# A two-layer decoder step: other places for the attention's products, the convolution's mean, the queries' normalisation and one parked slab

## What is computed

```python
x = x + 0.5 * swiglu_ffn(rmsnorm(x, ffn1_norm), w_gate, w_up, w_down)
cols = rmsnorm(x, mix_norm) @ w_in                       # 512 conv, 1152 attention, 640 rwkv
y_a = conv_module(glu(cols_a), conv_w, ...)              # 31 taps, layer norm over 256 channels, silu
y_b = combine_dilations(dilated attention over 3 groups) # samples: over cached windows wink, winv too
y_c, S = rwkv_time_mix(cols_c, prev, S0, ...)            # delta-rule recurrence, done in chunks
x = x + concat([y_a, y_b, y_c]) @ w_out
q = rmsnorm(x, xattn_norm) @ w_q
mk, mv = split(rmsnorm(mem, mem_norm) @ w_kv)            # samples use caches mem_k, mem_v instead
x = x + softmax(q mk^T / 16) mv @ w_o
x = x + 0.5 * swiglu_ffn(rmsnorm(x, ffn2_norm), ...)
```

## Time and profile before

| | |
|---|---|
| median of three runs | 1671.87 us |
| profiled execution | 1671.88 us |
| its span | 1670.1 us |
| PE busy | 1593.0 us (95%) |
| VectorE busy | 1074.7 us (64%) |
| ScalarE busy | 753.5 us (45%) |
| POOL busy | 207.1 us (12%) |
| transfers | 303.71 MB, 182 GB/s in the mean |

### The profile page before, as it was taken

One profiled execution on the slowest core, in us unless ns is written; L12 is line 12 of the kernel. 1 busy time (PEld: TensorE's weight loads), 2 busy tenths in 40 slices (PEclk: granted clock), 3 DMA queues, 4 the chain that ended last, 5 costly groups with the idle time before them and its releaser, 6 DMA issues.

```text
span 1670.1 us, 32138 instructions
## 1 busy us (share of the span) xinstructions
PE 1593.0 (95%) x13716; PEld 1507.9 (90%) x13716; DVE 1074.7 (64%) x1659; ACT 753.5 (45%) x1293; POOL 207.1 (12%) x190
## 2 busy tenths in 40 slices
PE   8999999999899989999999999998998998999997
PEld 8999999886689779999999999998767896999997
DVE  6776467878563367775477754779875642777744
ACT  5444348324444344443354433573355443544433
POOL 1000000980010010000010000029501000100000
PEclk9999999998999999999999999999979999999999
DMA  6666744303537665445445667442234477544541
GB/s 241 268 248 249 290 161 135 113 20 90 215 117 291 257 252 177 156 172 168 161 159 209 237 254 275 135 149 72 61 120 177 152 287 301 198 173 154 175 164 41
DMA packets 39965, 303.71 MB, mean 182 GB/s; under 512 B 4816, under 2 KB 4976, under 8 KB 7408
## 3 DMA queue, kind: packets, MB, share of 16 engines
q1 hardware_dynamic: 37488, 288.92, 47.8%
q0 software_dynamic: 2048, 11.17, 2.4%
q10 hardware_dynamic: 288, 1.57, 0.3%
HBM read 291.88 MB, written 36.83 MB: 197 GB/s over the span
## 4 chain that ended last, share of the span: by engine, by line
PE 79%; DVE 11%; ACT 5%; DMA 2%; issue 2%; SPq 0%; DVEq 0%; ACTq 0%
PE bank L676 22%; PE bank L678 22%; PE bank L677 21%; PE bank L860 3%; DVE w_lo L1911 3%; ACT w_hi L1385 1%; DMA slots<-stream 1%; ACT arena L1385 1%; PE bank L1285 1%; PE bank L1270 1%; DVE h_mem L1927 1%; PE bank L1339 1%; PE bank L1158 1%; PE bank L824 1%; PE bank L1322 1%
## 5 line engine op out<-in xcount | busy, mean ns | idle before, releaser
L1911 DVE TENSOR_TENSOR w_lo<-slots,w_hi 128x1024 fp32r<-128x1024 f32 x386 | 484.5, 1258 | 339.5 <-ACT w_hi L1385 338.5
L676 PE MATMUL bank<-h_hi,w_hi 128*128 128x288 f32 x1936 | 578.1, 299 | 18.3 <-DVE w_lo L1911 10.5
L677 PE MATMUL bank<-h_lo,w_hi 128*128 128x288 f32 x1936 | 571.9, 295 | 0.0
L678 PE MATMUL bank<-h_hi,w_lo 128*128 128x288 f32 x1936 | 570.0, 294 | 0.0
L1385 ACT CAST w_hi<-slots 128x1024 fp32r<-128x1024 f32 x390 | 406.4, 1046 | 290.0 <-PE bank L678 261.4
L676 PEld LDWEIGHTS bank<-h_hi,w_hi 128*128 128x128 f32 x1936 | 363.6, 188 | 25.9 <-DVE w_lo L1911 10.2
L678 PEld LDWEIGHTS bank<-h_hi,w_lo 128*128 128x128 f32 x1936 | 365.3, 189 | 0.0
L677 PEld LDWEIGHTS bank<-h_lo,w_hi 128*128 128x128 f32 x1936 | 364.3, 188 | 0.3
L678 PE MATMUL bank<-hid_hi,w_lo 128*128 128x288 f32 x704 | 207.7, 295 | 0.0
L677 PE MATMUL bank<-hid_lo,w_hi 128*128 128x288 f32 x704 | 207.3, 294 | 0.0
L676 PE MATMUL bank<-hid_hi,w_hi 128*128 128x288 f32 x704 | 207.1, 294 | 0.0
(11 more groups left out here) (334 smaller groups left out, 2115.6 us busy)
## 6 DMA issues: line engine op xcount, KB each, us to landing
slots<-stream SPq DMA_DIRECT2D x237, 1024.0 KB, 5.0
out_win3k<-win3k SPq DMA_DIRECT2D x2, 4080.0 KB
out_win3v<-win3v SPq DMA_DIRECT2D x2, 4080.0 KB
h_mem<-stream SPq DMA_DIRECT2D x4, 1024.0 KB, 10.6
out_win2k<-win2k SPq DMA_DIRECT2D x2, 2032.0 KB
out_win2v<-win2v SPq DMA_DIRECT2D x2, 2032.0 KB
con<-consts SPq DMA_DIRECT2D x1, 2340.0 KB, 10.8
arena<-mem_in POOLq DMA_DIRECT2D x2, 1024.0 KB, 5.6
```

What stands on the lines that cost most here:

```text
L676: mm(out, lhs[0], rhs[0], start=start, stop=False)
L677: mm(out, lhs[0], rhs[1], start=False, stop=False)
L678: return mm(out, lhs[1], rhs[0], start=False, stop=stop)
L1911: D(tt(out, src, hi.bitcast(F32), ALU.subtract), name)
```

## The change

- **Start.** SP loads only layer 0's gains first (half of those columns); the rest comes later, with the other constants. It waits for the first weights before it issues their second half, and for x's first part before it issues the constants. PE waits for these only ahead of the first sum of squares.
- **First feed-forward half.** Three units are split ahead of the root, not two.
- **In-projection.** On VectorE the norms of the keys come ahead of the decay part.
- **Solve.** The mean of the convolution runs on bank 2 in two parts inside the samples' solve, the first transposes of the values too.
- **Attention.** PE's and ScalarE's order is written out: a block's scores come between the transposes and the value products of the block before, and the memory's squares are eight and eight, between the last blocks (in bank 0). `p_rows` lies at another address, so its memset waits for a store and not for the last value products.
- **Out-projection.** `out1` comes behind `winv3` in `ORDER`; the splits of its two units stand within the memory's normalise, on ScalarE behind the copy of `s_out`.
- **Queries.** x times gain is split as `xq_hi`, `xq_lo` as the output tiles come, without the root; VectorE multiplies the root in at the eviction, in place of ScalarE's copies. POOL clears `qz`.
- **Values.** A fourth slab, `memv3`, is parked, in the place of the keys (`kx`), behind their store; `o0` comes behind `memv7`; the samples' values are read in the order 4, 5, 0, 1, 2, 3, 6, 7.

The core of the diff (`conv_mean` and `value_rows` hold the matmuls and transposes that stood in rows before):

```diff
+VALUE_ORDER = (4, 5, 0, 1, 2, 3, 6, 7)
...
-for _i, _next in ((0, ("wink", 0)), (1, ("winv", 1))):
-    ORDER.remove(("out", _i))
-    ORDER.insert(ORDER.index(_next), ("out", _i))
+ORDER.remove(("out", 0))
+ORDER.insert(ORDER.index(("wink", 0)), ("out", 0))
...
-PARKED = tuple(("memv", _i) for _i in range(3))
-PARKED_BEHIND = ("kv", 4)
-ORDER.remove(("o", 0))
-ORDER.insert(ORDER.index(("memv", 6)), ("o", 0))
+PARKED = tuple(("memv", _i) for _i in range(4))
+PARKED_BEHIND = {("kv", 4): (0, 1, 2), ("kv", 7): (3,)}
...
-            sp.dma_start(par_all[:, :, 0:gains], small[:, :, 0:gains]).then_inc(par_landed, 16)
+            sp.dma_start(par_all[:, 0, 0:gains], small[:, 0, 0:gains]).then_inc(par_landed, 16)
             sp.dma_start(x[:, 0:EARLY], x_in[:, 0:EARLY]).then_inc(x_landed[0], 16)
+            sp.wait_ge(unit_landed, 16)
             sp.dma_start(slots[:, 0, UNIT:], stream[0, 0, :, UNIT:]).then_inc(slab_landed[0], 16)
             sp.dma_start(x[:, EARLY:], x_in[:, EARLY:]).then_inc(x_landed[1], 16)
+            sp.wait_ge(x_landed[0], 16)
...
-                    if n == SLAB_AT[PARKED_BEHIND]:
-                        for i, dst in enumerate(parked):
-                            sp.wait_ge(tensor_done, TL.value(l, ("q", "cols", KT - 1) if i else ("xattn", "ss")))
-                            sp.dma_start(dst, stream[l, NSLAB + i]).then_inc(parked_landed[i], 16)
+                        sp.dma_start(par_all[:, 1:, 0:gains], small[:, 1:, 0:gains]).then_inc(con_landed, 16)
+                    for i in PARKED_BEHIND.get(ORDER[n], ()):
+                        reader = (("xattn", "ss"), ("q", "cols", KT - 1), ("q", "cols", KT - 1), ("xs", 7))[i]
+                        sp.wait_ge(tensor_done, TL.value(l, reader))
+                        if i == 3:
+                            sp.wait_ge(stored, store_value(l, "memk"))
+                        sp.dma_start(parked[i], stream[l, NSLAB + i]).then_inc(parked_landed[i], 16)
...
+                pool.wait_ge(vector_done, VL.value(l, ("x_out", 0)))
+                pool.wait_ge(stored, store_value(l, "wkv_s"))
+                PL.done(nc.gpsimd.memset(qz, 0.0), "qz_clear")
...
-            pe.wait_ge(start_landed, 16)
...
+                    if l == 0 and tag == "ffn1":
+                        pe.wait_ge(start_landed, 16)
...
+                    i = mm(bank[2][:, 0:T], ones, ycv[:, ch, :], start=ch == 0, stop=ch == 1)
...
                 TL.done(i, "s_y")
+                value_rows(0)
...
                 TL.done(i, ("r", 2))
+                conv_mean(0)
...
                 TL.done(i, ("u", 2))
+                conv_mean(1)
...
-                for u in range(5):
-                    if u < 4:
-                        scores(u)
-                        cache_scores(u)
-                    if u:
-                        apply_probs(u - 1)
-                sum_squares("mem", MEM, hm)
...
+                turn_probs(2)
+                memory_squares(range(4))
+                apply_probs(2)
+                turn_probs(3)
+                memory_squares(range(4, KT))
+                apply_probs(3)
...
-                columns("q", UNITS["q"], range(KT), (h_hi, h_lo), lambda k: (VL, ("xattn", "h_lo", k)), range(7), lambda t: (SL, ("qx", t)))
+                columns("q", UNITS["q"], range(KT), (xq_hi, xq_lo), lambda k: (VL, ("xattn", "x_lo", k)), range(7),
+                        lambda t: (VL, ("qx", t)))
...
-                sample_values(range(3))
+                sample_values(VALUE_ORDER[0:2])
...
-                sample_values(range(3, 6))
+                sample_values(VALUE_ORDER[2:6])
                 prompt_out(2)
-                sample_values(range(6, DEC_BATCH))
+                sample_values(VALUE_ORDER[6:])
...
-                    ahead = 2 if tag == "ffn1" else 0
+                    ahead = 3 if tag == "ffn1" else 0
...
-                for u in range(2, NW + 1):
-                    split(UNITS["out"] + u)
...
+                split(UNITS["out"] + NW - 1)
+                memory_hi(range(2, 5))
+                split(UNITS["out"] + NW)
+                memory_hi(range(5, 6))
...
-                rms("xattn", x, rs, T, out_done, lambda: split(next_unit(UNITS["out"] + KT - 1)), h_hi,
-                    lambda k: memory_keys(k // 4) if k % 4 == 0 else None)
-                for t in range(2, K_EARLY):
+                for k in range(KT):
+                    out_done(k)
+                    gained_hi(l, "xattn", k, "xattn", xq_hi)
+                    square("xattn", x, T, k)
+                split(next_unit(UNITS["out"] + KT - 1))
+                root("xattn", rs, T)
...
-                    act.wait_ge(tensor_done, TL.value(l, ("q", "cols", t)))
-                    copy(qx[:, t, :], bank[t % 7][:, 0:T])
-                    if t == 0:
-                        act.wait_ge(vector_done, VL.value(l, "qz_clear"))
-                    copy(qz_own[:, t], bt(bank[t % 7][:, TP:T]), ("qx", t))
...
-                dve.wait_ge(tensor_done, TL.value(l, ("attn", 3)))
+                dve.wait_ge(stored, store_value(l, "wkv_s"))
...
-                for u in range(2, NW + 1):
-                    split(UNITS["out"] + u)
...
-                normalise("mem", memx, hm, mem_rs, MEM, (hm_hi, hm_lo))
+                normalise("mem", memx, hm, mem_rs, MEM, (hm_hi, hm_lo),
+                          lambda k: split(UNITS["out"] + NW - 1 + (k == 6)) if k in (3, 6) else None)
...
-                dve.wait_ge(stored, store_value(l, "wkv_s"))
-                D(nc.vector.memset(qz, 0.0), "qz_clear")
+                    gained_lo(l, "xattn", t, "xattn", l, xq_hi, xq_lo, "x_lo")
...
-                normalise("xattn", x, h, rs, T, (h_hi, h_lo), lambda k: split(next_unit(kv_unit(k // 4))) if k in (0, 4) else None)
-                for t in range(2, K_EARLY):
+                dve.wait_ge(scalar_done, SL.value(l, ("xattn", "rms")))
+                D(nc.vector.reciprocal(rs[:], rs[:]))
...
+                    dve.wait_ge(tensor_done, TL.value(l, ("q", "cols", t)))
+                    if t == 0:
+                        settle()
+                    D(tt(qx[:, t, :], bank[t % 7][:, 0:T], rs[:], ALU.mult))
+                    if t == 0:
+                        dve.wait_ge(pool_done, PL.value(l, "qz_clear"))
+                    D(tt(qz_own[:, t], bt(bank[t % 7][:, TP:T]), bt(rs[:, TP:T]), ALU.mult), ("qx", t))
```

## The result

The changed kernel took 1654.69, 1659.43, 1661.75 and 1664.39 us; a fifth run of 2200.99 us, with a granted clock of 0.65, is left out. The kernel before took 1671.55 in the median of five (1671.07 to 1672.5). The ratio is 0.9927 with an interval of 0.9914 to 0.994, some 12 us (11 by the medians); the forecast was 1645, its range 1637 to 1658. The kernel is faster, but by less than half of what I summed, and its runs now lie up to 10 us apart, where those of before lie within 1.4 here (within 4.0 to 7.1 in the later measurements).

What follows compares the result with a forecast made beforehand. Bound: a stream of PE matmuls with holes (79% of the chain). Gains 1.4 + 0.8 + 2 x (0.6 + 5.1 + 4.0 + 2.5) = 26.6 us off span 1670.1, plus 1.8 outside, gave 1645 us; range 1637 to 1658.

Steps and rivals of the forecast that it cites:

- start: Kernel start: PE no longer waits for constants before its first matmul; 1.4 us gained once (0.6 to 2.1).
- three units ahead: First feed-forward half: third cast moves ahead of the root, removing a PE wait in layer 1; 0.8 us once (0 to 0.8).
- key norms: In-projection: swapping two pieces of VectorE's work gains nothing, unless POOL's taps start late.
- mean within the solve: Samples' solve: halves of the convolution mean fill PE's waits for ScalarE; 0.6 us a layer (-0.4 to 1.2).
- attention to out-projection: Attention, memory squares, out-projection: reordering covers PE's waits, less 0.9 given back; 5.1 us a layer, low end 2.0.
- queries: Query units: unnormalised x removes three PE holes waiting for VectorE; 4.0 us a layer (3.5 to 4.2).
- parked slab: Values: a fourth parked slab removes PE's waits for the last two value slabs; 2.5 us a layer (1.5 to 2.7).
- rival (d): Out-projection and keys: the new 3 us wait sends TensorE to its lower level; slower, 1675 us and up; 4%.
- rival (b): Solve and attention: the clock stays full, giving 1641 us; 14%.
- T near 435: Attention: sign that the transposes of the samples' probabilities, at 442.60 before, would start near 435 us.
- Rival (a): Out-projection: the new wait exceeds 3 us because `out1` shares transfer time, eating attention's gain; 1653 us; 18%.
- Rival (c): Queries: evictions or POOL's clearing hold a bank or unit, so the 4.0 us return as waits; 1653 us; 6%.

Runs made afterwards that it cites:

- keys_back: The changed kernel with VectorE's key norms behind the decay part again, as before: 1656.67 us, ratio 0.9884.
- before_mean: The kernel before plus only the split convolution mean and first value transposes inside the samples' solve: 1688.17 us, ratio 1.008.
- four_back: The changed kernel with mean, value transposes and key norms put back, SP's two start waits removed, samples' attention low half made earlier: 1643.42 us, ratio 0.9806.
- no_sp_waits: The changed kernel without SP's two waits at the start: 1656.65 us, ratio 0.9899.

## Why the prediction was wrong

Its own steps, in their order; shifts are those of PE's start of the same work between the two first profiles, layer 0 and layer 1.

| step | forecast, us a layer | measured |
|---|---|---|
| start (once) | 1.4 gained | 0.6 to 0.8 lost |
| three units ahead (once) | 0.8 gained | 1.0 gained |
| key norms | 0 | 0.76 lost in both, and in the chunk solve 0.7 more in layer 0 and 1.1 in layer 1, where a low stretch came (1140 to 1146) |
| mean within the solve | 0.6 gained | 4.6 and 1.9 lost |
| attention to out-projection | 5.1 gained | 6.3 and 6.0 gained |
| queries | 4.0 gained | 4.1 and 4.1 gained |
| parked slab | 2.5 gained | 3.0 and 3.3 gained |

Added up, the profiled run gains 17.5 us of span instead of 26.6. The terms that failed make 13 us of loss against the sum (2.0 of the start, 3.3 of the key norms with the chunk solve, 7.7 of the mean); the good ones give 4 back. The other runs of the changed kernel lose up to another 10, by their clocks nearly all of it at the lower level (0.976 in the profiled run, 0.97 in the slowest).

**The start failed** at the sentence that the two waits hold back only "slabs 1 to 4, of which none is waited for". The first thing behind the wait is the second half of the first unit, and behind it the rest of x; by ScalarE's order the second part of x is split behind both, and PE stood 3.41 us for it. The products that came earlier also ran at a slow pitch twice (7.96 to 10.7 and 14.59 to 18.0). I had traced what needs the constants, not what stands behind the waiting SP.

**Key norms at nothing failed** for the reason that I named and did not price: I looked for POOL's taps, while VectorE's lateness at the start of the chunk solve, for which PE waited 2.9 us before and 3.6 after, stood in the trace of before. Only the order on VectorE had changed ahead of it, but span x clock of keys_back shows no gain from putting it back.

**The mean within the solve** was the step that decided: entered at 0.6 gained a layer, it measured 4.6 and 1.9 lost. The holes closed, as before_mean shows at equal clock; the bounds of -0.4 to 1.2 held the holes alone. I had even computed that a half takes 1.15 us "at the clock of that row", took this low level as given, and never asked where it had ended before: within ten wide products in a row, which the edit takes apart, and with a wait of 0.56 us ahead of the six that are left. The forecast's rival (d) had the mechanism, a longer stretch at the lower level, in another place (behind the new wait, where the clock was 1.00 from 452 to 480 in the changed kernel), and rival (b) let the clock only get better. No rival had the one that came.

**Attention** went as argued in its waits, but 6.3 and 6.0 are not the 5.1 of the sum. The waits of the value products vanished, the spell from 416 came again (0.66 in 416 to 426 before and after), and with it my sum has 3.5 a layer. More came because the wait of 1.20 us ahead of the first transposes, which I had kept, went too (0.9 came back at layer 0's scores), and because less was given back. So the middle that I took came near by luck. The stall for the last value slab went, and the new wait, forecast at 3 us, is 2.1 and 2.3. From the samples' transposes to the attention part PE takes 16.9 us where it took 16.8: 0.1 given back (0.4 in layer 1) instead of 0.9. The mark that I gave, T near 435, was missed (442.86) since the solve ahead of it had lost what the attention then gained. Rival (a) did not come.

**Queries and values** came out by their rows (the values a little above their bound of 2.7): no wait at the first two units above 0.6 us, none for value slabs. Rival (c), evictions that hold up units, shows only as 0.9 us in three waits for casts.

On the clock the prediction weighed a rule of the Trainium skill (TensorE: Matmul & The Clock Gate, Part 1: The HAM clock gate), that the gate follows how busy PE has been recently, and the rule gave 1642. The trace does not bear that out as long as "busy" is read from the profile: PE is busy 15.45 of the 16 us from 396 to 412 in the changed kernel, and the clock is 0.50 and 0.59. The same section of the Trainium skill says that at a kernel's start the matmuls at the low level were 6, 11 or 14 in runs of one kernel. The traces agree: in the seven profiles with the same program at the start, the second group of products leaves the slow pitch between 17.2 and 21.1 us. In the middle of the kernel the level rose at 411 in one run of the changed kernel and at 403 in another.

The range failed with the same step. It took the cost of the lower level in the solve as fixed, although and the row of the mean showed it at work there; a low end of some -5 us a layer for any edit that reorders PE's work inside a low stretch would have put 1661 into it.

What stays open: why the level rises at different times in runs with the same instructions, why layer 1 lost less to it in the profiled run (1.9 against 4.6), and whether it is the missing wide products or the wait of 0.56 us ahead of the six that lets the low stretch run on.

## What to carry to other kernels

Where a trace shows TensorE at its lower level, look for the work in which the low stretch ends before moving any of it: here, filling waits of 0.6 us with halves of a wide block cost several us a layer, and leaving the block whole right ahead of the next wide one was better. When a queue gains a wait, list what stands behind it instruction by instruction, up to the first one that something needs. And multiply each run's span by its granted clock: if that product fell as forecast and the time did not, look for the missing gain in the clock before you doubt the sum of holes.

## What the hardware showed that I had not expected

- **Useless products that shorten a run.** Four extra matmuls, 2.29 us a layer at the lower level, brought a ratio of 0.9885 (0.9869 to 0.9902) where the kernel without them has 0.9927 (0.9914 to 0.994, and 0.9904 to 0.995 when measured again).
- **One edit, both signs.** Closing holes of about 0.6 us made a kernel slower by 13 us (before_mean, ratio 1.008), though at equal clock it was some 3 us shorter.
- **The first products are slow while the clock column shows 1.00.** In the kernel before, the products from 12 to 15.7 us follow each other at 0.24 us and those behind at 0.13, and the clock of that window reads 1.00. There the pitch of equal products, twice as long, looks like the lower level, and the column does not show it.
- **An earlier start can buy a second slow stretch, and the wait between does not tell whether.** In the changed kernel the products run at 0.24 from 7.96, stand for 3.41 us, and run at 0.24 again from 14.59 to 18.0. In four_back, with 0.86 us between, the second group runs at 0.13, but in no_sp_waits, with 0.74 between, at 0.24 again (14.0 to 17.4).
